# A running maximum for attention rows of over 1024 keys, with the rescale on GpSimd

## The chip, the core and the metric

The kernel runs on one core of a Trainium2 chip. A core has TensorE (PE in the profile; PEld is its weight load), VectorE (DVE), ScalarE (ACT), GpSimd (POOL) and SyncE (SP), which only issues transfers. The metric is the device time of one execution in microseconds. The kernel before takes 2585.28 us, the median of three runs (2584.13 to 2590.26). The profile was taken in an execution of its own, of 2582.51 us.

## What is computed

One layer of a hybrid encoder on 2048 tokens of width 1024, in float32: an attention branch and a gated linear recurrence on one projected input, merged by gates. The change touches the attention alone. It has 8 heads, 96 columns for queries and keys and 64 for values; a query sees all keys of its own chunk of 64 and of the earlier ones:

```python
sc = jnp.einsum('bhqd,bhkd->bhqk', qi, k).astype(jnp.float32) * scale
mask = key_chunk[None, :] <= qc[:, None]
sc = jnp.where(mask, sc, -jnp.inf)
p = jax.nn.softmax(sc, axis=-1).astype(v.dtype)
return jnp.einsum('bhqk,bhkd->bhqd', p, v)
```

## The kernel before

The kernel has five stages, one after another, with a barrier between them: input projection, merge logits and recurrence, the latent projections, attention, and merge with output. In each, every engine has its own written-out instruction list, and semaphores order them.

**Rows and chunks.** In `attention` a head's 2048 queries are 16 rows i of 128 queries each; four rows make a block b (TPB = 4, NB = 4). A row's keys come in chunks c of 512, b + 1 of them, the last cut at the diagonal. Rows 0 to 7 have up to 1024 keys and one piece of exponentials; rows 8 to 15 (blocks 2 and 3) have over 1024 keys and two pieces: piece 0 is chunks 0 and 1, 1024 columns, and piece 1 is the rest. LED = 8 is the first row with two pieces.

**One row.** TensorE (`queries`, L1651) computes each chunk of scores as three products of split operands (L66 to L68) into `scores`, which has four PSUM banks; before a chunk it waits until the piece that used this bank is exponentiated. VectorE (`maxima`, L1588) reduces each chunk to a column of `chunk_max` (L1592), these to `row_max` (L1595), and writes `neg_max` (L1601), the negative scaled maximum, into one of two columns by the parity of i. ScalarE (`exponentials`, L1530) waits for it before piece 0 (L1537), and writes exp(scale * score - maximum) to `probs[b]` in SBUF, with the sums of the piece in `sums` (L1541). Such an operation is followed in the profile by an ACTIVATION_READ_ACCUMULATOR, which delivers the sum.

**Tiles.** When a block's four rows are exponentiated, its probabilities are turned tile by tile: tile (b, j) is 128 keys by the block's queries. TensorE transposes it into one of three banks of `turn` (L1677), ScalarE rounds it into `pT` (`hi_part`, L1551), VectorE subtracts to get the low part (`lo_part`, L1608), and TensorE multiplies both by the values into `o_acc` (L1689, L1690). A finished block is copied to `oT` (L1565), turned (L1718), its halves are added (L1621), divided by the summed exponentials (`total`, `inv`) and stored (`o_out`, L1627).

**The order.** `attention_schedule` (L1358) gives 18 steps per head; each names a row, some tiles, a block to copy and a block to write out. Rows 8 to 11 go with the tiles of blocks 0 and 1, rows 12 to 15 with those of block 2, and rows 0 to 7 of the next head with those of block 3. In a step TensorE makes the row's scores, transposes this step's tiles and multiplies those of the step before; ScalarE rounds two tiles (AHEAD), does piece 0, rounds the rest and does piece 1; VectorE does the row's maxima, then the subtractions, then `outputs` of a block where there is one. The first tile of block 2, (2,0), is transposed in the step of row 12; that of block 3, (3,0), in the step of the next head's row 0, before which TensorE's scores of row 0 wait for all exponentials of this head. For block b, that first transpose waits for the last piece of the block's last row (L1673 to L1675). GpSimd only prepares two constants at the start of the stage and is then idle.

Of the kernel before, what the change touches and what calls it, by code (L numbers as in the profile page):

```python
# [7 lines left out]
ALU = mybir.AluOpType  # L8
ACT = mybir.ActivationFunctionType
# [4 lines left out]
P = 128  # L14
# [1364 lines left out]
def attention(nc, qT, knT, kpT, vTok, ident_d, oA):  # L1379
# [43 lines left out]
    with ExitStack() as ctx:  # L1423
# [19 lines left out]
        late_k = sb("late_k", [P, P], F32R)  # L1443
        mask_raw = sb("mask_raw", [P, 2, P])
        chunk_max = sb("chunk_max", [P, NB])
        row_max = sb("row_max", [P, 1])
        neg_max = sb("neg_max", [P, 2])
        sums = sb("sums", [P, NB, TPB, 2])
        total = sb("total", [P, TPB])
        inv = sb("inv", [P, TPB])  # L1450
# [11 lines left out]
        chunk_max_done = sem("chunk_max_done")  # L1462
        row_max_done = sem("row_max_done")
        max_ready = sem("max_ready")
        exp_done = sem("exp_done")
        turned = sem("turned")
        hi_ready = sem("hi_ready")
# [13 lines left out]
        with nc.Block() as block:  # L1481
# [37 lines left out]
            def _(pool):  # L1519
# [5 lines left out]
                pool.tensor_scalar(early_q[:], mask_raw[:, 0], 1.0, None, ALU.mult).then_inc(const_set, 1)  # L1525
                pool.tensor_scalar(late_k[:], mask_raw[:, 1], 1.0, None, ALU.mult).then_inc(const_set, 1)

            @block.scalar
            def _(act):
                def exponentials(h, i, piece):  # L1530
                    b, r = i // TPB, i % TPB
                    first, end = 2 * piece, min(2 * piece + 2, b + 1)
                    n = min(end * BLK, (i + 1) * P) - first * BLK
                    bank = s_bank(i, 0)
                    src = scores[:].rearrange("p b n -> p (b n)")[:, (bank + first) * BLK:(bank + first) * BLK + n]
                    if piece == 0:
                        act.wait_ge(max_ready, h * TT + (i + 1))  # L1537
                        if r == 0 and i < LED and not is_first(h):

                            act.wait_ge(turned, h * TURNS + (TURN_AT[b, TPB * (b + 1) - 1] + 1 - TURNS))  # L1540
                    act.activation(probs[b][:, r, first * BLK:first * BLK + n], src, ACT.Exp,  # L1541
                                   bias=neg_max[:, i % 2:i % 2 + 1], scale=SCALE,
                                   accum_out=sums[:, b, r, piece:piece + 1]).then_inc(exp_done, 1)

                def hi_part(h, tile):
# [41 lines left out]
            def _(dve):  # L1587
                def maxima(h, i):  # L1588
                    b = i // TPB
                    for c in range(b + 1):  # L1590
                        dve.wait_ge(qk_done, h * CHUNKS + (CHUNK_AT[i, c] + 1))
                        dve.reduce_max(chunk_max[:, c:c + 1], scores[:, s_bank(i, c), 0:width(i, c)], AX.X)\  # L1592
                           .then_inc(chunk_max_done, 1)
                    dve.wait_ge(chunk_max_done, h * CHUNKS + (CHUNK_AT[i, b] + 1))
                    dve.reduce_max(row_max[:], chunk_max[:, 0:b + 1], AX.X).then_inc(row_max_done, 1)  # L1595
                    dve.wait_ge(row_max_done, h * TT + (i + 1))
                    if not is_first(h) or i >= 2:
                        before = (i - 2) % TT
                        at = PIECE_AT[before, before // (2 * TPB)] - (PIECES if i < 2 else 0)
                        dve.wait_ge(exp_done, h * PIECES + (at + 2))  # L1600
                    dve.tensor_scalar(neg_max[:, i % 2:i % 2 + 1], row_max[:], -SCALE, None, ALU.mult).then_inc(max_ready, 1)  # L1601

                def lo_part(h, tile):
                    b, j = tile
# [6 lines left out]
                def outputs(h, b):  # L1611
                    at = TURN_AT["o", b]
                    n = h * NB + (b + 1)
                    if b >= 2:
                        dve.tensor_tensor(total[:], sums[:, b, :, 0], sums[:, b, :, 1], ALU.add).then_inc(total_ready, 1)
                    else:
                        dve.tensor_copy(total[:], sums[:, b, :, 0]).then_inc(total_ready, 1)
                    dve.wait_ge(total_ready, n)
                    dve.reciprocal(inv[:], total[:]).then_inc(inv_ready, 1)
                    dve.wait_ge(o_lo_ready, n)  # L1620
                    dve.tensor_tensor(o_sum[:], turn[:, at % 3].rearrange("p (t n) -> p t n", n=P)[:, :, 0:VD], o_lo[:],  # L1621
                                      ALU.add).then_inc(o_sum_ready, 1)
                    dve.wait_ge(o_sum_ready, n)
                    dve.wait_ge(inv_ready, n)
                    dve.sem_inc(turn_read, 1)
                    dve.wait_ge(o_stored[b % 2], h * 32 + (b // 2 * 16 + 16))
                    dve.tensor_tensor(o_out[:, b % 2], o_sum[:], inv[:].unsqueeze(2).to_broadcast([P, TPB, VD]), ALU.mult)\  # L1627
                       .then_inc(o_ready, 1)
# [21 lines left out]
            def _(pe):  # L1650
# [15 lines left out]
                def transposes(h, tile):  # L1666
# [6 lines left out]
                    if j == 0 or j >= TPB * b:  # L1673
                        i = TPB * b + (TPB - 1 if j == 0 else j - TPB * b)
                        pe.wait_ge(exp_done, h * PIECES + (PIECE_AT[i, i // (2 * TPB)] + 2))  # L1675
                    for r in range(max(0, j - TPB * b), TPB):
                        last = pe.transpose(turn[:, at % 3, r * P:(r + 1) * P], probs[b][:, r, j * P:(j + 1) * P], ident[:])  # L1677
                    last.then_inc(turned, 1)
# [478 lines left out]
```

## Time and profile before

| | before |
|---|---|
| median of three runs | 2585.28 us |
| profiled execution, span | 2582.51 us, 2580.7 us |
| mean granted TensorE clock | 0.943 |
| busy share PE, PEld, DVE, ACT, POOL | 88%, 73%, 44%, 35%, 16% |
| the attention stage's exponentials (L1541), first and last start | 1538.0 us, 2104.9 us |
| exponentials L1541 | 192, 166.9 us, 869 ns each |
| chunk maxima L1592 | 320, 184.0 us, 607 ns each |
| transposes L1677 | 1088, 152.7 us, 288 ns each |

The page gives for each group of instructions its line, engine, operation, the tile written and those read, the count, the busy time and the mean of one. "Idle before" is the time that the engine sat idle directly ahead of these instructions, with the one that ended it. Times in the rows by time are microseconds from the start of the span. Head 2's steps of rows 8 to 15 are at 1702 to 1745 us, and the other heads repeat them with nearly the same durations.

### The profile page before, as it was taken

How to read it: one execution, taken by the hardware profiler on the slowest of the kernel's cores; microseconds unless marked ns; L12 is line 12 of the kernel's file. 1: busy time of each engine (PE TensorE's matmuls, PEld its weight loads, DVE VectorE, ACT ScalarE, POOL GpSimd, SP SyncE). 2: the span in 40 equal slices, each digit the busy share in tenths (PEclk: the TensorE clock that was granted, in tenths of full speed). 3: DMA queues.
4: the chain of work that ended last, by engine and by line, in shares of the span. 5: the costliest groups of instructions: out<-in, count | busy, mean ns of one | idle time of the engine just before them, and what ended most of it. 6: DMA issues, size and time to landing. Idle time of an engine off the chain costs nothing. (4 is left out here: it accounts for less than half of the span.)

```text
span 2580.7 us, 34228 instructions
## 1 busy us (share of the span) xinstructions
PE 2275.6 (88%) x11680; PEld 1881.8 (73%) x11680; DVE 1127.4 (44%) x2016; ACT 911.7 (35%) x1676; POOL 423.4 (16%) x248
## 2 busy tenths in 40 slices
PE   6999999899699999999578948888888885889898
PEld 5888888688578888887456847777777764678776
DVE  5000000100044444444367746777777765554542
ACT  7111110101133433343441115555566653343431
POOL 1222241312011111111243200000000002411210
PEclk9999999999899999999679968999999996899999
DMA  5222221411222222221744460222221106563652
GB/s 177 74 73 73 73 77 33 147 69 53 87 80 93 89 90 93 89 90 62 243 148 132 116 175 12 64 65 63 65 62 36 39 10 225 165 182 123 192 160 68
DMA packets 228716, 256.06 MB, mean 99 GB/s; under 512 B 60272, under 2 KB 159344, under 8 KB 223728
## 3 DMA queue, kind: packets, MB, share of 16 engines
q1 hardware_dynamic: 203888, 208.11, 28.0%
q10 hardware_dynamic: 23616, 43.00, 4.4%
q0 software_dynamic: 1152, 4.19, 0.5%
q8 instruction: 32, 0.52, 0.1%
q14 instruction: 28, 0.23, 0.0%
HBM read 157.21 MB, written 98.04 MB: 99 GB/s over the span
## 5 line engine op out<-in xcount | busy, mean ns | idle before, releaser
L66 PE MATMUL bankD<-hT_hi,d_w_hi 128*128 128x512 f32 x512 | 213.0, 416 | 32.5 <-POOL d_w_lo L609 32.5
L1551 ACT ACTIVATE pT<-turn 128x512 fp32r<-128x512 f32 (+1 forms) x320 | 158.3, 532 | 198.5 <-PE turn L1677 198.1
L1608 DVE TENSOR_TENSOR pT<-turn,pT 128x512 fp32r<-128x512 f32 (+1 forms) x320 | 184.3, 606 | 73.8 <-ACT pT L1551 71.2
L66 PE MATMUL bankA<-hT_hi,w_hi 128*128 128x512 f32 x544 | 212.2, 390 | 0.0
L68 PE MATMUL bankA<-hT_hi,w_lo 128*128 128x512 f32 x544 | 211.7, 389 | 0.0
L67 PE MATMUL bankA<-hT_lo,w_hi 128*128 128x512 f32 x544 | 211.6, 389 | 0.0
L1592 DVE TENSOR_REDUCE chunk_max<-scores 128x1 f32<-128x512 f32 (+2 forms) x320 | 184.0, 607 | 59.7 <-PE scores L1663 44.5
L331 DVE TENSOR_TENSOR v_raw<-bankA,v_raw 128x512 fp32r<-128x512 f32 x16 | 11.0, 692 | 447.6 <-ACT v_raw L289 447.6
L66 PE MATMUL scores<-k_sb,q_sb 96*128 96x512 f32 (+2 forms) x320 | 130.3, 407 | 85.1 <-ACT probs L1541 48.4
L67 PE MATMUL bankD<-hT_lo,d_w_hi 128*128 128x512 f32 x512 | 201.7, 394 | 0.0
L68 PE MATMUL bankD<-hT_hi,d_w_lo 128*128 128x512 f32 x512 | 201.3, 393 | 0.0
L1541 ACT ACTIVATE probs<-scores,neg_max 128x1024 f32<-128x1024 f32 (+2 forms) x192 | 166.9, 869 | 44.2 <-DVE neg_max L1601 42.7
L66 PE MATMUL bankA<-wt_hi,hT_hi 128*128 128x512 f32 x384 | 153.0, 398 | 9.2 <-DVE v_raw L331 7.2
L1677 PE MATMUL turn<-ident_c,probs 128*128 128x128 f32 x1088 | 152.7, 288 | 1.7 <-ACT probs L1541 1.7
L67 PE MATMUL bankA<-wt_lo,hT_hi 128*128 128x512 f32 x384 | 151.3, 394 | 0.0
L68 PE MATMUL bankA<-wt_hi,hT_lo 128*128 128x512 f32 x384 | 151.3, 394 | 0.0
L66 PEld LDWEIGHTS scores<-k_sb,q_sb 96*128 96x128 f32 x320 | 64.1, 200 | 115.7 <-ACT probs L1541 64.1
L271 ACT ACTIVATE stage<-bankA 128x512 f32<-128x512 f32 x68 | 40.7, 598 | 301.6 <-PE bankA L68 300.1
L66 PEld LDWEIGHTS bankD<-hT_hi,d_w_hi 128*128 128x128 f32 x512 | 97.0, 189 | 56.5 <-issue 20.7
L1689 PE MATMUL o_acc<-pT,v_sb 128*128 128x512 f32 (+1 forms) x320 | 128.9, 406 | 8.8 <-ACT oT L1565 5.7
L66 PE MATMUL bankE<-e_uT,e_wb_hi 128*128 128x512 f32 x256 | 105.3, 411 | 31.4 <-POOL e_wb_lo L1888 29.8
L1677 PEld LDWEIGHTS turn<-ident_c,probs 128*128 128x128 f32 x1088 | 127.1, 149 | 4.3 <-DVE pT L1608 2.3
(224 smaller groups left out, 4925.6 us busy)
## 6 DMA issues: line engine op xcount, KB each, us to landing
projT<-stage ACTq DMA_DIRECT2D x68, 256.0 KB, 2.4
projT<-d_stage ACTq DMA_DIRECT2D x64, 256.0 KB, 2.4
e_l_in<-projT SPq DMA_DIRECT2D x64, 256.0 KB, 4.6
qT<-out_b SPq DMA_DIRECT2D x64, 192.0 KB, 2.2
q_sb<-qT SPq DMA_DIRECT2D x16, 768.0 KB, 10.3
w_raw<-in_w_in_dram SPq DMA_DIRECT2D x16, 512.0 KB, 4.5
hgTok<-v_raw SPq DMA_DIRECT2D x16, 512.0 KB, 2.6
gateTok<-stage ACTq DMA_DIRECT2D x32, 256.0 KB, 2.0
```

The source lines that it names most:

```text
L66: pe.matmul(out, a_hi, b_hi, start=first, stop=False)
L67: pe.matmul(out, a_hi, b_lo, start=False, stop=False)
L68: return pe.matmul(out, a_lo, b_hi, start=False, stop=last)
L271: act.activation(stage[:, blk], src, func).then_inc(bank_free, 1)
L331: dve.tensor_tensor(v_out[:, t % 2, :, 1], bank[:, t % 8].rearrange("p (h n) -> p h n", n=VD), v_out[:, t % 2, :, 0].bitcast(F32), ALU.sub ...
L1541: act.activation(probs[b][:, r, first * BLK:first * BLK + n], src, ACT.Exp, bias=neg_max[:, i % 2:i % 2 + 1], scale=SCALE, accum_out=sums[ ...
L1551: act.activation(pT[:, at % RING, 0, r0 * P:], turn[:, TURN_AT[tile] % 3, r0 * P:], ACT.Copy)\
L1592: dve.reduce_max(chunk_max[:, c:c + 1], scores[:, s_bank(i, c), 0:width(i, c)], AX.X)\
L1608: dve.tensor_tensor(pT[:, at % RING, 1, r0 * P:], turn[:, TURN_AT[tile] % 3, r0 * P:], pT[:, at % RING, 0, r0 * P:].bitcast(F32), ALU.subt ...
L1677: last = pe.transpose(turn[:, at % 3, r * P:(r + 1) * P], probs[b][:, r, j * P:(j + 1) * P], ident[:])
L1689: pe.matmul(dst, v_sb[:, u, j], pT[:, at % RING, 0, r0 * P:], start=j == 0, stop=False)
```

## The change

Rows 8 to 15 get a maximum per piece. After the first two chunks VectorE writes row_max and neg_max of piece 0 and ScalarE may exponentiate piece 0 by it. After the remaining chunks a second row_max, over all chunks, gives the neg_max of piece 1. ScalarE then computes `early_scale`, the exponential of the difference of the two, one column, ahead of piece 1. GpSimd multiplies the piece 0 of `probs` in place by it, 1024 columns, one instruction per row. TensorE's first transpose of blocks 2 and 3 waits for the rescales of the block's rows, and `outputs` multiplies the first sum by the scale before adding the second.

```diff
@@ gpsimd
+                with pool.Fori(0, HEADS) as h:
+                    for i in range(LED, TT):
+                        b, r = i // TPB, i % TPB
+                        pool.wait_ge(scale_ready, h * (TT - LED) + (i - LED + 1))
+                        pool.sem_inc(waited_pool, 1)
+                        pool.tensor_scalar(probs[b][:, r, 0:2 * BLK], probs[b][:, r, 0:2 * BLK], early_scale[:, b, r:r + 1], None,
+                                           ALU.mult).then_inc(rescaled, 1)
@@ scalar, exponentials
-                    if piece == 0:
-                        act.wait_ge(max_ready, h * TT + (i + 1))
+                    act.wait_ge(max_ready, h * PIECES + (PIECE_AT[i, piece] + 1))
+                    if piece == 1:
+                        act.activation(early_scale[:, b, r:r + 1], neg_max[:, i % 2, 0:1], ACT.Exp,
+                                       bias=neg_max[:, i % 2, 1:2], scale=-1.0).then_inc(scale_ready, 1)
+                    else:
                         if r == 0 and i < LED and not is_first(h):
 
                             act.wait_ge(turned, h * TURNS + (TURN_AT[b, TPB * (b + 1) - 1] + 1 - TURNS))
                     act.activation(probs[b][:, r, first * BLK:first * BLK + n], src, ACT.Exp,
-                                   bias=neg_max[:, i % 2:i % 2 + 1], scale=SCALE,
+                                   bias=neg_max[:, i % 2, piece:piece + 1], scale=SCALE,
@@ vector, maxima
-                    for c in range(b + 1):
...
+                    for piece in range(b // 2 + 1):
+                        end = min(2 * piece + 2, b + 1)
+                        for c in range(2 * piece, end):
+                            dve.wait_ge(qk_done, h * CHUNKS + (CHUNK_AT[i, c] + 1))
+                            dve.reduce_max(chunk_max[:, c:c + 1], scores[:, s_bank(i, c), 0:width(i, c)], AX.X)\
+                               .then_inc(chunk_max_done, 1)
+                        dve.wait_ge(chunk_max_done, h * CHUNKS + (CHUNK_AT[i, end - 1] + 1))
+                        dve.reduce_max(row_max[:, piece:piece + 1], chunk_max[:, 0:end], AX.X).then_inc(row_max_done, 1)
+                        dve.wait_ge(row_max_done, h * PIECES + (PIECE_AT[i, piece] + 1))
...
+                        dve.tensor_scalar(neg_max[:, i % 2, piece:piece + 1], row_max[:, piece:piece + 1], -SCALE, None, ALU.mult)\
+                           .then_inc(max_ready, 1)
@@ vector, outputs
                     if b >= 2:
-                        dve.tensor_tensor(total[:], sums[:, b, :, 0], sums[:, b, :, 1], ALU.add).then_inc(total_ready, 1)
+                        dve.tensor_tensor(total[:], sums[:, b, :, 0], early_scale[:, b], ALU.mult).then_inc(early_sum, 1)
+                        dve.wait_ge(early_sum, h * 2 + (b - 1))
+                        dve.tensor_tensor(total[:], total[:], sums[:, b, :, 1], ALU.add).then_inc(total_ready, 1)
@@ tensor, transposes
                         pe.wait_ge(exp_done, h * PIECES + (PIECE_AT[i, i // (2 * TPB)] + 2))
+                    if j == 0 and b >= 2:
+                        pe.wait_ge(rescaled, h * (TT - LED) + (b - 1) * TPB)
```

The order of the instructions themselves changes at these places. VectorE, the maxima of a row of block 3 (four chunks), before:

```order
L1592 TENSOR_REDUCE chunk_max<-scores 128x1
L1591 REGISTER_ALU
L1592 TENSOR_REDUCE chunk_max<-scores 128x1
L1591 REGISTER_ALU
L1592 TENSOR_REDUCE chunk_max<-scores 128x1
L1591 REGISTER_ALU
L1592 TENSOR_REDUCE chunk_max<-scores 128x1
L1595 TENSOR_REDUCE row_max<-chunk_max 128x1
L1596 REGISTER_ALU
L1600 REGISTER_ALU
L1601 TENSOR_SCALAR neg_max<-row_max 128x1
```

And the same row in the change (the REGISTER_ALU rows compute the value of a wait):

```order
L1610 TENSOR_REDUCE chunk_max<-scores 128x1
L1609 REGISTER_ALU
L1610 TENSOR_REDUCE chunk_max<-scores 128x1
L1613 TENSOR_REDUCE row_max<-chunk_max 128x1
L1614 REGISTER_ALU
L1619 TENSOR_SCALAR neg_max<-row_max 128x1
L1609 REGISTER_ALU
L1610 TENSOR_REDUCE chunk_max<-scores 128x1
L1609 REGISTER_ALU
L1610 TENSOR_REDUCE chunk_max<-scores 128x1
L1613 TENSOR_REDUCE row_max<-chunk_max 128x1
L1619 TENSOR_SCALAR neg_max<-row_max 128x1
```

A row_max and a neg_max stand after the second chunk, ahead of the third and the fourth. ScalarE in the step of row 14, from piece 0 to piece 1, before:

```order
L1541 ACTIVATE probs,sums<-scores,neg_max 128x1024
L1549 REGISTER_ALU
L1550 REGISTER_ALU
L1551 ACTIVATE pT<-turn 128x512
L1541 ACTIVATE probs,sums<-scores,neg_max 128x896
```

And in the change:

```order
L1557 ACTIVATE probs,sums<-scores,neg_max 128x1024
L1565 REGISTER_ALU
L1566 REGISTER_ALU
L1567 ACTIVATE pT<-turn 128x512
L1549 REGISTER_ALU
L1551 ACTIVATE early_scale<-neg_max 128x1
L1557 ACTIVATE probs,sums<-scores,neg_max 128x896
```

The one-column exponential stands between the third tile and piece 1. TensorE in the change, from the last chunk of the next head's row 0 (L1684 is its mask product) to the first tiles of block 3:

```order
L1684 MATMUL scores<-late_k,early_q 128x128
L1693 REGISTER_ALU
L1696 REGISTER_ALU
L1698 REGISTER_ALU
L1700 MATMUL turn<-ident_c,probs 128x128 x4
L1693 REGISTER_ALU
L1700 MATMUL turn<-ident_c,probs 128x128 x4
L1712 MATMUL o_acc<-pT,v_sb 128x384
```

The matmuls keep their order; the third register row (L1698) is the new wait for GpSimd ahead of the four transposes of tile (3,0).

## Rows read from the trace of the kernel before

**Rows 1.** Waits in 1500 to 2125 us: total, times, longest (us).
```profile
PE scores L66 <- ACT probs L1541: 48.4, 33, 1.9
ACT pT L1551 <- PE turn L1677: 198.1, 133, 3.9
```

**Rows 2.** Groups by shape, 1500 to 2125 us: busy us, mean ns, idle before.
```profile
L1541 ACT ACTIVATE probs<-scores,neg_max 128x1024 f32<-128x1024 f32 x80 | 89.2, 1115 | 11.6 <-DVE neg_max L1601 10.7
```

**Rows 3.** ScalarE by time, rows 14, 15: start, length, line, operation, idle.
```profile
1735.29 1.09 ACT L1551 ACTIVATE pT<-turn 128x512 fp32r<-128x512 f32 x2 [1.89 <-PE turn L1677]
1737.22 1.11 ACT L1541 ACTIVATE probs<-scores,neg_max 128x1024 f32<-128x1024 f32 x1 [0.85 <-DVE neg_max L1601]
1738.23 0.19 ACT L1541 ACTIVATION_READ_ACCUMULATOR probs<-scores,neg_max 128x1 f32 x1
1738.81 1.01 ACT L1541 ACTIVATE probs<-scores,neg_max 128x896 f32<-128x896 f32 x1
...
1744.18 1.11 ACT L1541 ACTIVATE probs<-scores,neg_max 128x1024 f32<-128x1024 f32 x1
```

**Rows 4.** TensorE by time: tile (2,0); row 15's chunks; tile (3,0).
```profile
1722.14 0.84 PE L1677 MATMUL turn<-ident_c,probs 128*128 128x128 f32 x6
...
1738.48 0.50 PE L66 MATMUL scores<-k_sb,q_sb 96*128 96x512 f32 x1 [1.05 <-ACT probs L1541]
...
1739.97 0.48 PE L66 MATMUL scores<-k_sb,q_sb 96*128 96x512 f32 x1
...
1745.99 1.72 PE L1677 MATMUL turn<-ident_c,probs 128*128 128x128 f32 x7
```

**Rows 5.** ScalarE by time, row 11: rounded tiles, piece 0, piece 1.
```profile
1717.45 0.77 ACT L1551 ACTIVATE pT<-turn 128x384 fp32r<-128x384 f32 x2 [1.75 <-PE turn L1677]
1718.31 1.12 ACT L1541 ACTIVATE probs<-scores,neg_max 128x1024 f32<-128x1024 f32 x1
...
1719.58 0.69 ACT L1541 ACTIVATE probs<-scores,neg_max 128x512 f32<-128x512 f32 x1
```

**Rows 6.** VectorE by time, maxima and subtractions of row 14.
```profile
1734.37 2.35 DVE L1592 TENSOR_REDUCE chunk_max<-scores 128x1 f32<-128x512 f32 x4
1736.75 0.16 DVE L1595 TENSOR_REDUCE row_max<-chunk_max 128x1 f32<-128x4 f32 x1
1737.03 0.15 DVE L1601 TENSOR_SCALAR neg_max<-row_max 128x1 f32<-128x1 f32 x1
...
1738.95 0.69 DVE L1608 TENSOR_TENSOR pT<-turn,pT 128x512 fp32r<-128x512 f32 x1 [0.56 <-ACT pT L1551]
```

**Rows 7.** ScalarE line of another stage: ns min/median/max, first, last.
```profile
L1968 ACT ACTIVATE e_std<-e_ss,e_eps x16: 294/295/296, 2247.6 to 2573.4; 128x1 f32<-128x1 f32 x16
```

**Rows 8.** GpSimd groups: tensor_scalar at 1024 and 128, memset at 1024.
```profile
L207 POOL TENSOR_SCALAR w_hi<-w_raw 128x1024 fp32r<-128x1024 f32 x17 | 47.1, 2773 | 282.7 <-PE bankA L68 271.2 <-DMA w_raw<-in_w_in_dram 11.1 <-POOL w_lo L209 0.4
L1525 POOL TENSOR_SCALAR early_q<-mask_raw 128x128 fp32r<-128x128 f32 x1 | 0.5, 532 | 0.1
L597 POOL MEMSET d_masked<- 128x1024 f32 x1 | 1.0, 951 | 0.0
```

**Rows 9.** ScalarE, GpSimd, VectorE by time, last stage.
```profile
2181.69 1.04 ACT L1926 ACTIVATE e_wb_hi<-e_wb_raw 128x1024 fp32r<-128x1024 f32 x1
...
2182.82 2.35 POOL L1888 TENSOR_TENSOR e_wb_lo<-e_wb_raw,e_wb_hi 128x1024 fp32r<-128x1024 f32 x1 [3.42 <-ACT e_wb_hi L1926]
...
2185.14 2.82 POOL L1901 TENSOR_TENSOR e_wo_lo<-e_y,e_wo_hi 128x1024 fp32r<-128x1024 f32 x1
...
2185.76 2.75 DVE L1990 TENSOR_TENSOR e_u<-e_sg,e_o_in 128x512 f32<-128x512 f32 x1
```

**Rows 10.** GpSimd and VectorE by time, latent projections.
```profile
1404.76 2.13 POOL L1131 TENSOR_SCALAR wq_hi<-wq_raw 128x768 fp32r<-128x768 f32 x1 [12.26 <-PE bankB L68]
...
1404.78 1.34 DVE L1284 TENSOR_TENSOR out_b<-turned,out_b 96x512 fp32r<-96x512 f32 x1 [0.70 <-ACT out_b L1211]
```

**Rows 11.** The stretch after row 15: length, busy by engine, granted clock.
```profile
1745.40:1749.00 3.60, 3.56 (x18) 3.57 (x19) 1.62 (x5) 1.20 (x2) 0.00 (x0) 0.56 0.00 0
```

More of the change, by code:

```diff
@@ L1445, in attention @@
         chunk_max = sb("chunk_max", [P, NB])
-        row_max = sb("row_max", [P, 1])
-        neg_max = sb("neg_max", [P, 2])
+        row_max = sb("row_max", [P, 2])
+        neg_max = sb("neg_max", [P, 2, 2])
+        early_scale = sb("early_scale", [P, NB, TPB])
         sums = sb("sums", [P, NB, TPB, 2])
@@ L1464, in attention @@
         max_ready = sem("max_ready")
+        scale_ready = sem("scale_ready")
+        rescaled = sem("rescaled")
+        early_sum = sem("early_sum")
+        waited_pool = sem("waited_pool")
         exp_done = sem("exp_done")
@@ L1589, in maxima @@
                     b = i // TPB
-                    for c in range(b + 1):
[L1591 to L1601, printed above, removed]
+                    for piece in range(b // 2 + 1):
[7 more added lines that the diff above has]
+                        dve.wait_ge(row_max_done, h * PIECES + (PIECE_AT[i, piece] + 1))
+                        if piece == 0 and (not is_first(h) or i >= 2):
+                            before = (i - 2) % TT
+                            at = PIECE_AT[before, before // (2 * TPB)] - (PIECES if i < 2 else 0)
+                            dve.wait_ge(exp_done, h * PIECES + (at + 2))
+                        dve.tensor_scalar(neg_max[:, i % 2, piece:piece + 1], row_max[:, piece:piece + 1], -SCALE, None, ALU.mult)\
+                           .then_inc(max_ready, 1)
                 def lo_part(h, tile):
```

## Prediction

> **What bounds the kernel now.** The page puts TensorE at 88% of the span, and its slices 24 to 33 are the attention stage, the only place that the change touches. I first read who waited for whom in that stage, then the groups by shape, then the time-ordered rows of one head (head 2, counted from 0, 1702 to 1775 us).
>
> The waits [rows 1] say that TensorE's own idle time there is short and comes mostly from ScalarE's exponentials (48.4 us), while ScalarE waits 198.1 us for transposes. Nobody holds the stage alone; a loop does. In each step TensorE makes the scores of row i, then transposes; ScalarE rounds two transposed tiles, exponentiates piece 0 of row i, and only that frees the banks for row i+1. The rows of head 2 show it: TensorE's first score matmul of row 15 starts at 1738.48 [rows 4], 0.06 us after ScalarE's piece 0 of row 14 ended at 1738.42 [rows 3].
>
> Does that piece wait for the maximum, which is what the change shortens? Seldom. Of all exponentials 1024 wide, 80 of them, ScalarE idled 10.7 us for neg_max in total [rows 2], and row 14 of one head alone has 0.85 us of it [rows 3], so 6.8 us over eight heads. Row 7's exponential is also 1024 wide and its code is unchanged. In row 11 the tile before ends at 1718.22 and the piece starts at 1718.31 [rows 5]. In the other rows over 1024 keys the piece starts when ScalarE itself is free.
>
> **What the change saves.** In row 14 VectorE is late, because it has just written out a block. Its four reduces take 2.35 us from 1734.37, so the spacing is 0.55 and the second ends at 1735.61; row_max follows after 0.04 and neg_max ends 0.43 after that starts [rows 6]: 1736.08 instead of 1737.18. ScalarE's second rounded tile ends at 1736.38, and ScalarE starts an operation 0.10 us and more before the last one ends (the accumulator read starts at 1738.23, the exponential ends at 1738.33) [rows 3]. With 0.12 for that, piece 0 could start at 1736.26, 0.96 us earlier. Other heads lose slightly less; I take 0.90. Row 11 can give 0.20 by the same overlap. Eight heads: 8 x 1.10 = 8.8 us gained, at best.
>
> **What it adds on ScalarE.** One exponential of one column before each piece 1. Its kind is not in this stage; the 128x1 activation elsewhere takes 295 ns [rows 7], less the 0.12 overlap 0.18 us. Bounds: 0.09 (a 0.19 us accumulator read less an overlap of 0.10) and 0.30. In row 14 piece 1 frees the third bank just in time: it starts at 1738.81, takes 1.01 and an accumulator read of 0.19, and the third chunk starts at 1739.97 [rows 3, 4]. There it costs 0.16 x 8 = 1.3 us. In rows 8 to 13 piece 1 is narrower and its end leaves TensorE room. In row 15 it is inside the next term.
>
> **What it adds on VectorE.** A row_max and a neg_max in the middle of each of 64 rows: 0.04 + 0.43 less 0.08 overlap and 0.09 that the next reduce would have overlapped, 0.48 us a row, 31 us in all. It is hidden: the piece 0 no longer waits for what comes after it, and after the two subtractions VectorE idles 0.56 us for the third tile [rows 6]. If that cover were gone it would cost at most those 31 us. The extra add for the sums of blocks 2 and 3 is two operations and a wait, 0.28 us; in block 2 it delays rows 2 and 3, whose exponentials VectorE does hold, but ScalarE then waits for transposes anyway: 1 us in total, bounds 0 and 2.2.
>
> **What it adds on GpSimd, and through it on TensorE.** This is the term that decides. Each of 64 rows gets one GpSimd tensor_scalar of 128x1024 float32. The nearest rows are exactly that operation and size, only into fp32r and with a constant: 2773 ns each, and 0.53 us at 128 columns [rows 8], that is 2.5 ns a column. I take 2.77. From below the nearest is the memset of 1024 columns, 0.95 us [rows 8]; from above I know nothing that excludes more for the per-row scalar, and put 3.3 as an estimate (the row plus a fifth).
>
> GpSimd was empty here, so 48 of the 64 have steps of time to spare: TensorE waits for them only at tile 0 of blocks 2 and 3, for rows 8 to 11 and 12 to 15. What decides is the last row of each, 16 in all. The chain is: scale ends 0.12 after piece 1 starts, GpSimd starts 0.09 later (as after ScalarE's rounding, 2182.73 to 2182.82) [rows 9], 2.77, and 0.06 to TensorE: 3.04 us after piece 1 starts, and piece 1 itself starts 0.18 later than now.
> Row 15: piece 1 starts at 1744.18 [rows 3] and the transposes of tile (3,0) at 1745.99 [rows 4], 1.81 us later. Late by 0.18 + 3.04 - 1.81 = 1.41 us, 8 times: 11.3 us.
> Row 11: piece 1 starts at 1719.58 [rows 5], the transposes of tile (2,0) at 1722.14 [rows 4], 2.56 us later. Late by 0.66 us, 8 times: 5.3 us.
> Queued behind the waiting transpose are all of TensorE's other transposes and value products of that step; ScalarE and VectorE wait for those. I find no later wait that gives it back.
>
> The GPSIMD Engine Reference of the Trainium skill, section 4.1 (Engine selection), says that a one-input operation on GpSimd is roughly line-rate. By that rule the rescale would take about 1.1 us as an estimate and both lateness terms would vanish. The 2773 ns row speaks against it.
>
> **A shared port.** VectorE operations that read two SBUF tensors are held by GpSimd here: e_u 128x512 took 2.75 us, ending 0.55 after GpSimd's own operation (2187.96) [rows 9], where 512 columns else take 0.69 [rows 6]. Under a GpSimd tensor_scalar it is shorter: out_b started 0.02 after wq_hi and ended at 1406.12, when wq_hi still ran until 1406.89 [rows 10]. Reduces and the subtractions read PSUM and are not in that class. In the change the small copy of the sums and o_out of block 1 come within 2.5 us after row 13's piece 1 starts, so they fall into row 13's rescale. I take 0.5 us of delay for VectorE, of which row 14's new slack covers 0.18: 0.3 x 8 = 2.6 us of the gain is lost. Bounds 0 and 7.7 (all of row 14's gain).
> SBUF — State Buffer of the Trainium skill, section Who interferes with whom, says the loser blocks for the whole instruction. By it the delay would be near 1.3 us and the loss 7.7; the out_b row contradicts it for a GpSimd tensor_scalar.
>
> **The clock.** After the idle time before row 0 of head 3 the granted clock was 0.56 in 1745.4 to 1749, most of it at the lower level, 1.2 GHz [rows 11]. The idle ahead of it grows by 1.4 us, so more heads may see the lower level there. Such a stretch costs up to half of its 3.6 us; I add 3 us, bounds 0 and 8.
>
> **Sum.** 11.3 + 5.3 + 1.3 + 2.6 + 1.0 + 3.0 - 8.8 = +15.7 us. The profiled execution took 2582.51 us, so 2598.2; the median of the runs is 2.8 above it, so 2601. About 0.3% (7.8 us) is what a measurement can tell from no change.
>
> **Rivals.**
> A: the rescale is short enough to be hidden (1.0 to 1.8 us). For it: the memset runs at 0.93 ns a column, and the output is plain float32, not fp32r. Against it: both sizes of the same operation, at 2.5 ns a column. Then no lateness and no port trouble: 1.4 (row 15's scale) + 1.3 + 1.0 - 8.8 = -5.1, or 2580. This is also the case on the other side: faster if the mechanism at row 14 gives its whole 0.96 us; it decides as soon as the rescale is under about 1.6 us (1.81 less 0.18 is what TensorE leaves). With 2.0 to 2.3 us it comes out within 0.3%, some 2583 to 2587.
> B: VectorE becomes the late one. Held until the rescale's end in the copy and again in o_out, it would start row 14's reduces over 2 us late, and piece 0 of row 14 would wait longer than now. Then +7.7 - 2.6 and up to 8 more for the later start: 2606 to 2614. For it: the held operations [rows 9, 10]. Against: out_b's early release.
> C: the change does not do what it says, since piece 0 is held by ScalarE's order and not by the maximum. For rows 8, 9, 10, 12 and 13 that is so, and it is in the forecast. Were it so in row 14 too, the gain of 7.2 us would be gone and with it the 2.6 lost from it: 2606.
>
> **Chances.** Forecast 0.58 (its own range 2592 to 2609), A 0.20, a rescale in between 0.12, B 0.10. Of the forecast 0.06 falls within 0.3%, all of the in-between does, and of A two thirds. Faster 0.07, same 0.31, slower 0.62. The range 2580 to 2611 leaves out half of A and the end of B.
>
> **What would show it.** In the profile after: a group of 64 GpSimd tensor_scalars, near 2770 ns; TensorE waiting on GpSimd 16 times, 0.6 to 0.7 us in eight and 1.4 in eight, at the transposes; ScalarE's neg_max wait in row 14 gone or down to 0.3; 64 one-column activations near 0.3 us. Wrong if the GpSimd group is under 1.9 us, if the transposes do not wait for it, or if VectorE's o_out is held beyond a microsecond.

## The result, and the profile after

| | before | after |
|---|---|---|
| median (range), 5 runs each | 2584.13 us (2578.39 to 2590.26) | 2608.89 us (2607.30 to 2610.63) |
| ratio | | 1.0098, 95% interval 1.0082 to 1.0113 |
| profiled execution, span | 2582.51 us, 2580.7 us | 2608.89 us, 2607.1 us |
| mean granted TensorE clock | 0.943 | 0.938 |
| busy share of GpSimd | 16% | 23% |

The change makes the kernel slower by 24.8 us, where 15.7 us were forecast: 2608.9 us instead of 2601. That lies 0.1 us inside the forecast's own range (2592 to 2609) and in the wider one (2580 to 2611). The sign, the place and the mechanism are as forecast; one term, the clock, was much larger and lies outside its own bounds.

**The groups that the change adds or moves.** First the page of the profile after (line, engine, operation, tile, count, busy us, mean ns, idle before):

```profile
L1538 POOL TENSOR_SCALAR probs<-probs,early_scale 128x1024 f32<-128x1024 f32 x64 | 182.2, 2846 | 432.2 <-ACT early_scale L1551 432.2
```

Then the groups by shape in 1500 to 2125 us, which answer [rows 2]:

```profile
L1557 ACT ACTIVATE probs<-scores,neg_max 128x1024 f32<-128x1024 f32 x79 | 88.3, 1118 | 3.6 <-DVE neg_max L1619 3.6
L1551 ACT ACTIVATE early_scale<-neg_max 128x1 f32<-128x1 f32 x63 | 19.3, 306 | 0.0
L1619 DVE TENSOR_SCALAR neg_max<-row_max 128x1 f32<-128x1 f32 x192 | 29.5, 154 | 10.0 <-DVE row_max L1613 1.1
```

The rescale (GpSimd's multiplication of piece 0) takes 2.85 us, near the 2.77 taken from the operation of the same size [rows 8]. ScalarE's idle time for the maximum ahead of a 1024-wide piece fell from 10.7 to 3.6 us: the change does what it says. The waits of the same stretch (total us, times, longest), against [rows 1]:

```profile
PE scores L66 <- ACT probs L1557: 41.5, 30, 1.8
PE turn L1700 <- POOL probs L1538: 14.2, 15, 1.3
PEld turn L1700 <- POOL probs L1538: 13.2, 12, 1.4
```

The last two are new: TensorE waits for GpSimd. The two are the matmul's and the weight load's sides of the same waits, not to be added. One by one the 16 waits are 0.62 to 0.75 us ahead of tile (2,0), 1.24 to 1.31 us ahead of tile (3,0), and 3.73 us in the last head.

**One wait, step by step.** ScalarE, GpSimd and TensorE by time in head 2, row 15 and the next head's row 0 (start us, length us; the counterparts are [rows 3] and [rows 4]):

```profile
1748.88 1.12 ACT L1557 ACTIVATE probs<-scores,neg_max 128x1024 f32<-128x1024 f32 x1
1749.88 0.21 ACT L1557 ACTIVATION_READ_ACCUMULATOR probs<-scores,neg_max 128x1 f32 x1
1749.97 0.29 ACT L1567 ACTIVATE pT<-turn 128x128 fp32r<-128x128 f32 x1
1750.13 0.31 ACT L1551 ACTIVATE early_scale<-neg_max 128x1 f32<-128x1 f32 x1
1750.31 1.13 ACT L1557 ACTIVATE probs<-scores,neg_max 128x1024 f32<-128x1024 f32 x1
...
1750.64 2.84 POOL L1538 TENSOR_SCALAR probs<-probs,early_scale 128x1024 f32<-128x1024 f32 x1 [2.57 <-ACT early_scale L1551]
...
1751.59 0.33 PE L66 MATMUL scores<-k_sb,q_sb 96*128 96x128 f32 x1 [1.76 <-ACT probs L1557]
1751.98 0.32 PE L1684 MATMUL scores<-late_k,early_q 128*128 128x128 f32 x1
1753.54 1.97 PE L1700 MATMUL turn<-ident_c,probs 128*128 128x128 f32 x8 [1.24 <-POOL probs L1538]
1755.16 0.67 PE L1712 MATMUL o_acc<-pT,v_sb 128*128 128x384 f32 x1
```

The scale ends at 1750.44, GpSimd starts 0.20 later (0.09 was forecast), ends at 1753.48, and the transposes start 0.06 after that: 3.23 us after the start of piece 1, where 1.81 were spent before. Note the lengths at the end: transposes of about 0.25 us each, at half speed.

**The clock there.** Windows of TensorE (length; busy by engine; the granted clock is the third number from the end), row 14, row 15, rows 0 and 1 of the next head, and the whole low stretch; they answer [rows 11]:

```profile
1738.56:1744.41 5.85, 5.71 (x35) 4.56 (x33) 5.16 (x12) 3.96 (x10) 2.85 (x1) 1.00 0.10 22
1744.41:1751.59 7.18, 5.42 (x26) 3.95 (x26) 6.00 (x15) 4.91 (x12) 3.80 (x2) 1.00 0.00 0
1751.59:1756.69 5.10, 3.86 (x18) 3.67 (x19) 1.73 (x5) 1.19 (x2) 1.89 (x1) 0.55 0.00 0
1756.69:1760.38 3.69, 3.69 (x22) 3.46 (x22) 2.00 (x6) 2.56 (x7) 0.00 (x0) 0.70 0.00 0
...
1752.00:1758.80 6.80, 5.56 (x27) 5.38 (x26) 2.71 (x8) 2.21 (x6) 1.48 (x1) 0.50 0.00 0
```

TensorE idles 1.76 us ahead of row 0's scores and another 1.24 us at the wait, and 6.8 us run at 1.2 GHz. Rows 0 and 1 of the same head before, 6.41 us instead of 8.79:

```profile
1745.43:1749.11 3.68, 3.67 (x19) 3.68 (x19) 1.74 (x5) 1.20 (x2) 0.00 (x0) 0.56 0.00 0
1749.11:1751.84 2.73, 2.73 (x22) 2.51 (x22) 1.79 (x6) 2.39 (x7) 0.00 (x0) 0.97 0.00 0
```

Before, a stretch of 3.4 us at half speed followed row 15 in four of seven heads and none in three; after, one of 6.8 us in each of the seven.

**Where the time went.** From the timeline, each row's step is the time from its first score matmul to the next row's. Summed over the heads (row 15: seven heads, since the last has no successor), in us. The first head's rows 0 to 7 stand ahead of the loop, without tiles; of its rows 0 and 1, 1.8 us are in each number of "0+1". "Half" is the time in the stage at the lower clock, 21 to 28 us of it in the stage's first rows in every kernel. This table also holds the experiments of the next section.

| kernel | stage | 8+9 | 12 | 13 | 14 | 15 | 0+1 | 7 | half |
|---|---|---|---|---|---|---|---|---|---|
| before | 563.2 | 87.0 | 52.9 | 48.6 | 52.8 | 48.7 | 41.7 | 42.1 | 69.8 |
| after | 584.1 | 83.4 | 59.3 | 50.4 | 46.7 | 50.4 | 64.3 | 41.5 | 100.6 |
| 1 scratch | 561.9 | 86.0 | 52.6 | 53.6 | 46.6 | 50.3 | 43.3 | 41.4 | 82.5 |
| 2 operations only | 567.8 | 88.7 | 53.1 | 48.9 | 58.6 | 50.7 | 35.4 | 41.4 | 58.6 |
| 3 split rescale | 560.0 | 87.4 | 52.6 | 53.6 | 46.4 | 50.4 | 40.1 | 41.4 | 79.6 |
| 4 filler at the wait | 582.0 | 82.4 | 59.2 | 58.2 | 46.4 | 50.3 | 55.3 | 41.5 | 86.2 |
| 5 kept busy | 579.6 | 92.6 | 59.3 | 55.2 | 46.5 | 50.3 | 45.8 | 41.5 | 86.8 |
| 6 row 14 only | 561.9 | 86.0 | 52.9 | 50.3 | 45.5 | 51.0 | 44.9 | 42.1 | 79.4 |
| 7 all but 11, 15 | 568.0 | 87.7 | 52.9 | 52.1 | 47.0 | 52.0 | 44.9 | 42.1 | 85.4 |
| 8 before, fillers | 566.1 | 92.1 | 52.9 | 45.5 | 52.9 | 48.6 | 35.4 | 49.1 | 55.8 |
| 9 split, fillers | 567.9 | 93.3 | 60.6 | 45.1 | 46.7 | 50.3 | 35.4 | 47.9 | 56.2 |
| 10 row 14, fillers | 560.3 | 88.5 | 52.9 | 45.5 | 45.4 | 51.0 | 35.4 | 51.9 | 51.4 |
| 11 row 14, one filler | 560.3 | 93.7 | 52.9 | 50.3 | 45.5 | 51.0 | 35.4 | 42.1 | 77.7 |

After less before: row 12 +6.4, rows 0 and 1 +22.6, row 15 +1.7, row 13 +1.8, row 14 -6.1, row 11 -1.0, rows 8 and 9 -3.6, the rest -0.9: +20.9. Behind the last row 15 the kernel takes 487.6 us where it took 481.4; the last head's wait is in that. In experiments 1, 2, 3 and 6 to 11, which have no such wait or a shorter one, it is 480.8 to 484.7, so some 3 us of the 6.2 can be scatter.

### The profile page after: what moved, and what is told of

It reads as the page before. It is cut to its first block and busy times, and to the rows that moved or that the text cites. A ratio compares the mean times of both kernels' runs of the same rounds, so it can differ in the third digit from the quotient of the medians.

```text
span 2607.1 us, 34783 instructions
## 1 busy us (share of the span) xinstructions
PE 2292.2 (88%) x11680; PEld 1893.3 (73%) x11680; DVE 1152.1 (44%) x2160; ACT 921.7 (35%) x1740; POOL 606.2 (23%) x312
## 5 line engine op out<-in xcount | busy, mean ns | idle before, releaser
L1538 POOL TENSOR_SCALAR probs<-probs,early_scale 128x1024 f32<-128x1024 f32 x64 | 182.2, 2846 | 432.2 <-ACT early_scale L1551 432.2
L66 PE MATMUL scores<-k_sb,q_sb 96*128 96x512 f32 (+2 forms) x320 | 131.6, 411 | 78.6 <-ACT probs L1557 41.5
L1700 PE MATMUL turn<-ident_c,probs 128*128 128x128 f32 x1088 | 161.6, 299 | 17.9 <-POOL probs L1538 17.9
L1700 PEld LDWEIGHTS turn<-ident_c,probs 128*128 128x128 f32 x1088 | 134.1, 155 | 22.6 <-POOL probs L1538 13.2
L1911 POOL TENSOR_TENSOR e_wb_lo<-e_wb_raw,e_wb_hi 128x1024 fp32r<-128x1024 f32 x32 | 76.1, 2379 | 293.0 <-ACT e_wb_hi L1949 293.0
```

Source lines behind the costliest of these rows:

```text
L66: pe.matmul(out, a_hi, b_hi, start=first, stop=False)
L1538: pool.tensor_scalar(probs[b][:, r, 0:2 * BLK], probs[b][:, r, 0:2 * BLK], early_scale[:, b, r:r + 1], None, ALU.mult).then_inc(rescaled, 1)
L1911: pool.tensor_tensor(wb_lo[:, u], wb_raw[:, u], wb_hi[:, u].bitcast(F32), ALU.subtract).then_inc(wb_ready, 1)
```

## Experiments

**Is it the wait? (1 scratch).** GpSimd does the same multiplications but writes to a buffer of its own, so piece 0 is not rescaled; TensorE's wait moves from a block's first tile to its fifth, where it is long over. GpSimd also waits for its own last multiplication (not shown).

```diff
-   pool.tensor_scalar(probs[b][:, r, 0:2 * BLK], probs[b][:, r, 0:2 * BLK], early_scale[...], None, ALU.mult)
+   pool.tensor_scalar(scaled_c[:], probs[b][:, r, 0:2 * BLK], early_scale[...], None, ALU.mult)
-   if j == 0 and b >= 2:
+   if j == TPB and b >= 2:
```

> The change with GpSimd's products written to a buffer of their own (so piece 0 isn't rescaled), and TensorE's wait for them moved from tile 0 to tile 4 of blocks 2 and 3. All instructions of the change remain, only nobody waits. Theory W (TensorE's 16 waits for the last rows' rescales, and the lower clock that follows them, are the whole loss): 3 to 7 us faster than before (row 14's 0.8 us in eight heads, less some 1.5 us of ScalarE's extra operation), the clock after row 15 as before. Rival P (GpSimd holds VectorE on the shared port, and the 31 us of added VectorE work come through): still at least 8 us slower than before.

Measured: 2581.03 us against 2586.46 for before on the same chip, ratio 0.9975 (0.9965 to 0.9985), inside theory W's 3 to 7 us. All of ScalarE's, VectorE's and GpSimd's new work is there, and the kernel is faster than before:

```profile
L1541 POOL TENSOR_SCALAR scaled_c<-probs,early_scale 128x1024 f32<-128x1024 f32 x64 | 182.0, 2844 | 410.9 <-ACT early_scale L1554 410.9
L1554 ACT ACTIVATE early_scale<-neg_max 128x1 f32<-128x1 f32 x64 | 19.6, 306 | 0.0
```

So the loss hangs on TensorE's wait for the rescale and what follows from it, and not on the added instructions by themselves; what the shared port costs is within the gain that is left. The multiplications are not in place here, which leaves it open whether that matters; their length, 2844 ns, is the same.

**What is the earlier start worth? (2 operations only).** As 1, but piece 0 waits for the row's last maximum again.

```diff
-   act.wait_ge(max_ready, h * PIECES + (PIECE_AT[i, piece] + 1))
+   act.wait_ge(max_ready, h * PIECES + (PIECE_AT[i, i // (2 * TPB)] + 1))
```

> As the kernel with the products in a buffer of their own, but piece 0 waits for the row's last maximum, so that the added operations remain and the early start is gone; output wrong in the same way. Theory W: against that kernel later by the early start at row 14, which is now 0.8 us plus VectorE's added 0.5 us and the held copy's 0.7 us, eight times: 8 to 16 us; against before +3 to +10 us. If the early start were worth nothing (rival C of the prediction), both kernels would be equal within 3 us.

Measured: 2595.12 us, ratio 1.0035 (1.0022 to 1.0049), inside both ranges of theory W: 14.1 us later than 1, 8.7 later than before. The row of the 1024-wide pieces:

```profile
L1560 ACT ACTIVATE probs<-scores,neg_max 128x1024 f32<-128x1024 f32 x80 | 89.1, 1114 | 18.4 <-DVE neg_max L1622 17.9
```

17.9 us of idle time for the maximum instead of 3.6, and row 14 takes 58.6 us instead of 46.6. The added operations are free only because the earlier start covers them: without it they make row 14 5.8 us longer than before, with it the row is 6.2 shorter. The 14 us between 1 and 2 are both together. Experiment 2 shows something of the clock too: TensorE idles 1.8 us ahead of row 0's scores as in the other kernels, and yet no half-speed stretch follows in any of the seven heads (rows 0 and 1: 35.4 us). The length of that idle time alone does not decide.

**Can the wait be avoided? (3 split rescale).** For rows 11 and 15 the rescale is cut in two, 384 and 640 columns; tile 0 waits for the first, tile 3 for the second. Everything is computed.

```diff
-   pool.tensor_scalar(probs[b][:, r, 0:2 * BLK], ...).then_inc(rescaled, 1)
+   for c0, c1 in ((0, 3 * P), (3 * P, 2 * BLK)) if r == TPB - 1 else ((0, 2 * BLK),):
+       pool.tensor_scalar(probs[b][:, r, c0:c1], probs[b][:, r, c0:c1], ...).then_inc(rescaled, 1)
-   if j == 0 and b >= 2:
-       pe.wait_ge(rescaled, h * (TT - LED) + (b - 1) * TPB)
+   if j in (0, 3) and b >= 2:
+       pe.wait_ge(rescaled, h * 2 * (TPB + 1) + (b - 2) * (TPB + 1) + (TPB if j == 0 else TPB + 1))
```

> The change with the rescale of rows 11 and 15 cut in two, 384 and 640 columns; tile 0 waits for the first part alone, tile 3 for the second. The first part takes about 1.2 us (2.5 ns a column and 0.2), ends 1.5 us after piece 1 starts, ahead of both tiles. Theory W: all waits go, 3 to 7 us faster than before. Rival P: at least 8 us slower than before.

Measured: 2581.85 us, ratio 0.9987 (0.9976 to 0.9999), 3.4 us by the ratio, as theory W had it. The parts take 1.24 and 1.89 us (1.2 was expected for the first). GpSimd by time at the same place as above, the waits of TensorE for it:

```profile
1742.85 3.10 POOL L1539 TENSOR_SCALAR probs<-probs,early_scale 128x384 f32<-128x384 f32 x2 [2.57 <-ACT early_scale L1552]
```

```profile
PE turn L1701 <- POOL probs L1539: 2.1, 1, 2.1
```

One wait is left of sixteen, the last head's, which has no scores of a next row 0 ahead of it (3.73 us in the change); row 12 is back at 52.6 us and rows 0 and 1 at 40.1. The same arithmetic with a shorter first instruction turns +24.8 us into a gain of 0.1%, less than the 0.3% that the prediction took for the least that a measurement tells; the interval here, of 11 runs against 21, just leaves out no change.

**How much is the clock? (4 filler at the wait, 5 kept busy).** Fillers are transposes of the identity into the bank that the step's first tile overwrites. Experiment 4 puts 6 (block 2) or 10 (block 3) ahead of the wait for GpSimd:

```diff
    if j == 0 and b >= 2:
+       for n in range(10 if b == 3 else 6):
+           pe.transpose(turn[:, at % 3, n % TPB * P:(n % TPB + 1) * P], ident[:], ident[:])
        pe.wait_ge(rescaled, h * (TT - LED) + (b - 1) * TPB)
```

> The change with TensorE filling its wait for GpSimd: 6 transposes of the identity at tile (2,0), 10 at tile (3,0), into the bank that the tile's own transposes overwrite. The waits stay as long, the idle time ahead of the tiles goes. Theory W with the clock as its larger half: the half-speed stretches after row 15 (6.8 us in each head) go or halve, 7 to 14 us faster than the change, +11 to +18 us against before. Rival (the stretches come from other idle time, such as that ahead of row 0's scores, or cost nothing): like the change, +25 us.

Measured: 2604.92 us, ratio 1.0074 (1.0062 to 1.0086): 0.24% below the change's 1.0098, the expectation's lower edge not reached. The half-speed stretch after row 15 became 3.4 us instead of 6.8, and rows 0 and 1 fell by 9.0 us. But row 13 rose by 7.8, since a half-speed stretch now fell there in every head:

```profile
1730.31:1737.54 7.23, 7.23 (x35) 6.11 (x36) 5.00 (x11) 3.73 (x9) 2.85 (x1) 0.76 0.00 0
```

Experiment 5 keeps the ten at block 3 only and adds 12 ahead of row 0's scores, so that both idle times around row 0 are filled (the ten are not shown again).

```diff
+   if i in (0,) and at is not None:
+       pe.wait_ge(turn_read, h0 * TURNS + (at - 1))
+       for m in range(12):
+           pe.transpose(turn[:, at % 3, m % TPB * P:(m % TPB + 1) * P], ident[:], ident[:])
```

> The changed kernel with TensorE kept busy in its two idle stretches around the end of row 15: 12 identity transposes ahead of the scores of the next head's row 0 and 10 ahead of the wait for GpSimd at tile (3,0), into the bank that this step's first tile overwrites. The rescale and both waits stay. Theory K (the piece of the loss that the forecast sized too small is the half-speed stretch that follows the longer idle, about 1.8 us a head of the 3.2 us by which rows 0 and 1 grew): those rows fall from 8.9 us to about 7.0 to 7.2 in every head that has both fillers, and the kernel takes 12 to 16 us less than the change, 2593 to 2597, unless another row turns to half speed. Rival L (the loss is the wait itself): rows 0 and 1 stay at 8.9 us and the time within 4 us of the change, 2605 or more.

Measured: 2600.29 us, ratio 1.0047 (1.0031 to 1.0062). TensorE by time, then rows 0 and 1 as windows:

```profile
1746.09 1.53 PE L1679 MATMUL turn<-ident_c 128*128 128x128 f32 x12 [0.28 <-DVE pT L1627]
1747.59 0.33 PE L66 MATMUL scores<-k_sb,q_sb 96*128 96x128 f32 x1
...
1748.09 1.28 PE L1703 MATMUL turn<-ident_c 128*128 128x128 f32 x10
1749.54 1.09 PE L1707 MATMUL turn<-ident_c,probs 128*128 128x128 f32 x8 [0.17 <-POOL probs L1538]
```

```profile
1747.58:1751.23 3.65, 3.48 (x30) 3.24 (x29) 0.89 (x4) 0.92 (x2) 1.90 (x1) 1.00 0.00 0
1751.23:1753.88 2.65, 2.65 (x23) 2.42 (x22) 2.46 (x7) 2.56 (x8) 0.00 (x0) 1.00 0.00 0
```

The wait is still there, its end still set by GpSimd, and eight transposes now take 1.09 us instead of 1.97. Rows 0 and 1 take 6.29 us a head instead of 8.79 (head 2 to 3), the same within 0.02 us in all seven heads; in the table 45.8 against 64.3 us. That is below the 7.0 to 7.2 expected. With the wait unchanged and the clock at 1.00, 18.5 us of the change's time in these rows was the lower clock. The stage as a whole is only 4.5 us shorter, because rows 8 and 9 rose by 9.2 and row 13 by 4.8, to half-speed stretches there: row 13 has one in six of eight heads instead of three. By the ratios the kernel gained 0.51%, by the medians of two chips 8.6 us. The theory that the clock is the missing part holds for the rows it names; its number for the whole, 2593 to 2597, was missed for the reason it had reserved.

**Which rows carry the gain? (6 row 14 only, 7 all but 11 and 15).** The running maximum is restricted to some rows; the others have one maximum and no rescale.

```diff
+ RUNNING = (14,)
...
-   for i in range(LED, TT):
+   for i in RUNNING:
...
-   for piece in range(b // 2 + 1):
+   for piece in range(b // 2 + 1 if i in RUNNING else 1):
```

> The change for row 14 alone: the other rows over 1024 keys have one maximum for both pieces as before, and block 2 has no rescale. Theory W: row 14's start 0.8 us earlier in eight heads, less 0.1 for ScalarE's operation, and no wait for GpSimd: 4 to 7 us faster than before. Rival (the early start is given back in row 15): within 2 us of before.

Measured: 2581.78 us against 2586.21 for before (second chip), ratio 0.9985 (0.9974 to 0.9997), 4 us as theory W had it. Eight of the 64 running maxima give as much as all of them with the split rescale (0.9987): row 14 takes 45.5 us instead of 52.8. A part goes to row 15, +2.3, and to rows 13, 0 and 1.

With `RUNNING = (8, 9, 10, 12, 13, 14)`:

> The running maximum for rows 8, 9, 10, 12, 13 and 14; rows 11 and 15, the last of their blocks, keep one maximum and need no rescale. Theory W (the loss sits in the rescales of the last rows alone, and the other rows' operations are hidden): the gain at row 14 stays, and the time is that of the split rescale, 2579 to 2584. Rival Q (the operations of all rows cost something that a late rescale hid): 2586 or more.

Measured: 2590.48 us against 2587.48 (third chip), ratio 1.0009 (0.9999 to 1.0018). Rival Q's number came, not W's. The row of the 1024-wide pieces shows one reason:

```profile
L1565 ACT ACTIVATE probs<-scores,neg_max 128x1024 f32<-128x1024 f32 x80 | 89.2, 1115 | 6.7 <-DVE neg_max L1627 5.7
```

The 2.1 us above the change's 3.6 are row 15, some 0.30 a head: it now waits for a maximum over all four chunks, while VectorE comes late from row 14's additional operations. Against experiment 3, row 15 is 1.6 us longer, row 11 1.1, and rows 0 and 1 4.8, these by the clock. The running maximum of the other rows has no gain of its own in this table, and row 14's operations delay VectorE for row 15.

**Can the clock be had back by itself? (8 to 11).** 12 fillers each ahead of the scores of rows 0, 9 and 13, where TensorE idled before, put into the kernel before, into 3 and into 6; at last into 6 ahead of row 0 alone. The edit is that of experiment 5, with `i in (0, 9, 13)` for 8 to 10.

> The kernel before, with 12 transposes of the identity on TensorE ahead of the scores of rows 0, 9 and 13, where it idles 1.7 us in every head; they write the bank that the next tile overwrites. Theory W with its clock part (half-speed stretches follow these idles, 0.9 us a head after row 15, 1.0 at row 9 and 0.4 at row 13): 8 to 20 us faster than before, granted clock 0.955 or more. Rival (the stretches have another cause, or the fillers delay TensorE): no faster than before.

Measured: 2582.66 us, ratio 0.9982 (0.9969 to 0.9995), 3.6 us faster where 8 to 20 were expected, with a granted clock of 0.950 where 0.955 or more was: a miss in size. Rows 0, 1, 9 and 13 are at full clock in nearly all heads; rows 0 and 1 are the reference for full speed, 4.82 us a head:

```profile
1746.07:1748.23 2.16, 2.16 (x18) 2.16 (x19) 0.89 (x4) 0.92 (x2) 0.00 (x0) 1.00 0.00 0
1748.23:1750.89 2.66, 2.66 (x23) 2.43 (x22) 2.46 (x7) 2.57 (x8) 0.00 (x0) 1.00 0.00 0
```

They saved 6.3 us in rows 0 and 1, 10.3 in row 9 and 3.1 in row 13, and lost 15.4 in row 8 and 7.0 in row 7. TensorE by time at the end of row 7 of head 4, and the window of row 8:

```profile
1840.90 0.66 PE L1722 MATMUL turn<-ident_c,oT 128*128 128x128 f32 x4 [0.72 <-ACT oT L1565]
1845.54 0.79 PE L66 MATMUL scores<-k_sb,q_sb 96*128 96x512 f32 x1 [3.97 <-issue]
```

```profile
1845.54:1853.49 7.95, 7.52 (x32) 6.54 (x32) 3.56 (x8) 2.81 (x7) 0.00 (x0) 0.54 0.98 221
```

TensorE stood 3.97 us without any wait that the profile shows ("issue"), where the loop over the heads turns, and 4.41 us at the turn before (head 2), and ran at half speed after it. In this one profiled execution the stage is 2.9 us longer than before, while the median of 12 runs is 3.6 below that of 35: the rows tell where the time moves, not how large the whole is in other executions. What holds TensorE there was not tried.

> The rescale of rows 11 and 15 cut in two, and the same 12 transposes ahead of rows 0, 9 and 13. Theory W: the two gains add, 12 to 25 us faster than before.

Measured: 2588.24 us, ratio 1.0011 (1.0000 to 1.0022), a clear miss. To the losses in rows 7 and 8 comes row 12, 60.6 us instead of 52.6: the fillers ahead of row 13's scores wait for VectorE to read their bank, and that comes 1.49 us after TensorE's last product instead of 0.50 in experiment 8, so they end too late. TensorE by time at the end of head 3's row 12:

```profile
1798.06 1.53 PE L1680 MATMUL turn<-ident_c 128*128 128x128 f32 x12 [1.49 <-DVE pT L1628]
1799.34 0.48 PE L66 MATMUL scores<-k_sb,q_sb 96*128 96x512 f32 x1
```

VectorE is later there by the added row_max and neg_max and by o_out, 0.81 us instead of 0.43, of which below.

> The running maximum for row 14 alone, and the same 12 transposes ahead of rows 0, 9 and 13. Theory W: the two gains add, 12 to 26 us faster than before, as the split one or slightly better.

Measured: 2580.91 us, ratio 0.9976 (0.9964 to 0.9987), 5.3 us faster where 12 to 26 were expected. A miss in size too; row 7 takes 51.9 us, with 5.5 us of TensorE standing at each of the two turns.

> The running maximum for row 14 alone, with 12 identity transposes ahead of the scores of row 0 only; none ahead of rows 9 and 13. With the fillers ahead of rows 0, 9 and 13 in the kernel before, rows 7 and 8 grew by more than 1 us a head; theory M: that is the longer instruction list at the loop's turn and half speed there, so a third of the fillers keeps rows 0 and 1 at 4.8 us and leaves rows 7 and 8 near 5.6 and 4.8: 7 us less than row 14 alone, about 2575. Rival N: any filler moves the half-speed stretch to another row, and the time stays near 2581.

Measured: 2578.98 us against 2587.48, ratio 0.9966 (0.9953 to 0.9979). With a third of the fillers row 7 is back at 42.1 us, as theory M had it, and rows 0 and 1 keep their 35.4; rows 8 and 9 rose to 93.7 by half-speed stretches there, which is rival N's. The time lies between theory M's 2575 and rival N's 2581. It is the fastest complete version run, faster than both kernels (its profiled execution, 2585.30, was its slowest); against 6 alone the intervals overlap.

## Why the prediction was right, and where its size was off

The chain that it put first, the two last rescales that TensorE waits for, is what the runs show. That the total lies within the range owes something to the range's width: the clock term alone is 7.4 us above its forecast.

**The rescale's price.** 2.77 taken, 2.85 measured. Rival A, the short rescale, fails by it. The estimate of 1.1 us by the rule of the GPSIMD Engine Reference of the Trainium skill, section 4.1 (Engine selection), fails too, against 2.85.

**Lateness of rows 11 and 15.** Forecast 0.66 and 1.41 us a head, 16.6 in all. Row 12's step grew by 0.80 a head, 6.4 in all. For row 15 the clean measure is experiment 5 against 8, both at full clock: 3.65 us against 2.16 in row 0, 1.49 a head, 11.9 for eight. Together 18.3. The chain was right link by link; only GpSimd's start (0.20 for 0.09) and its length were short.

**ScalarE's scale.** 0.306 us ([rows 7] have 0.295) with 0.13 of it overlapped: piece 1 starts 0.22 after the end of piece 0's accumulator read instead of 0.06. Forecast 1.3 us; row 15's step is 1.7 longer in seven heads.

**The gain, and the shared port.** Forecast -7.2 in row 14 and -1.6 in row 11, with 2.6 given back to the port: -6.2. Measured -6.1 and -1.0: -7.1. VectorE by time, between the subtractions and row 14's maxima, answers [rows 6]; GpSimd's rescale runs from 1739.27 to 1742.12:

```profile
1739.53 0.88 DVE L1638 COPY total<-sums 128x4 f32<-128x4 f32 x1
1740.44 0.18 DVE L1640 RECIPROCAL inv<-total 128x4 f32<-128x4 f32 x1
...
1741.11 0.43 DVE L1648 TENSOR_TENSOR o_out<-o_sum,inv 128x256 f32<-128x256 f32 x1 [0.19 <-DVE o_sum L1642]
1741.46 1.28 DVE L1610 TENSOR_REDUCE chunk_max<-scores 128x1 f32<-128x512 f32 x2
1742.77 0.15 DVE L1613 TENSOR_REDUCE row_max<-chunk_max 128x1 f32<-128x2 f32 x1
1742.96 0.15 DVE L1619 TENSOR_SCALAR neg_max<-row_max 128x1 f32<-128x1 f32 x1
1743.06 1.16 DVE L1610 TENSOR_REDUCE chunk_max<-scores 128x1 f32<-128x512 f32 x2
```

The copy was held, 0.88 us instead of 0.16; o_out was not, 0.43 us in the middle of the rescale. It also matters when they start. In all eight heads block 1's copy starts 0.26 us after the rescale's start and ends 1.13 to 1.14 us after it; block 0's copy ends as its rescale starts and takes 0.16. In experiment 3 o_out of block 0 starts 0.17 to 0.25 us after the start of the 640-column part, and there it is held too, in all eight heads, until 1.07 us after that start. GpSimd, then VectorE, in experiment 3:

```profile
1717.41 3.10 POOL L1539 TENSOR_SCALAR probs<-probs,early_scale 128x384 f32<-128x384 f32 x2 [1.51 <-ACT early_scale L1552]
1718.89 0.81 DVE L1649 TENSOR_TENSOR o_out<-o_sum,inv 128x256 f32<-128x256 f32 x1 [0.27 <-DVE o_sum L1643]
```

In the change neg_max ends at 1743.11 and piece 0 starts at 1743.15, right behind ScalarE's rounded tiles: the delay just fitted in. In experiment 6, where row 13 is not rescaled and the copy takes 0.16 us, row 14 takes 45.5 us over the heads instead of 46.7: the held copy costs at most 1.2 us, where 2.6 were forecast. Rival B, VectorE as the late one, fails. The rule that the loser blocks for the whole instruction (SBUF — State Buffer of the Trainium skill, section Who interferes with whom) agrees with neither row: the copy was let go 1.72 us before the rescale's end. Rival C fails in row 14: without the earlier start it takes 12 us more (experiments 1 and 2).

**The clock: the step that was mis-sized.** The prediction put "3 us, bounds 0 and 8" for more heads at the lower level; measured are 10.4, outside these bounds. Rows 0 and 1 lost 6.3 us to it before (41.7 less 35.4 at full speed, experiment 8) and 18.5 after (64.3 less 45.8, experiment 5): +12.2 in seven heads. Rows 8 and 9 gave back 3.6, and row 13 added 1.8: 10.4 us in all, from one profiled execution of each kernel. How many heads have a stretch after row 15 varies without the wait as well: rows 0 and 1 lose between nothing (experiment 2) and 9.5 us (6) to it. The working reckoned with one stretch of 3.6 us as in [rows 11], in more heads, and capped it at half of its length. It took the new wait for a longer idle time ahead of the stretch ("grows by 1.4 us"). It is a second one, of 1.24 us, that comes four matmuls, 0.7 us, after the first one of 1.76. With both the stretch is 6.8 us in all seven heads, where four of seven had one of 3.4; with the second one filled (experiment 4) it is 3.4 us in all seven, with both filled (5) there is none.

**The sum by rows of the trace.** Lateness 18.3, clock 10.4, scale 1.9, gain -7.1, small rows -0.9: +22.6, and the scatter behind the stage. The terms forecast were 16.6, 3.0, 1.3, -6.2 and +1.0 for the outputs. The last did not show: rows 2 to 6 have the same steps as before within 0.02 us.

What stays open: why an idle time of 1.8 us is followed by a half-speed stretch in some heads and not in others, why the stretches move to rows 8, 9 and 13 when they are filled at row 0, and what holds TensorE at the loop's turn in experiment 8.

## What to carry to other kernels

Of 64 hidden operations the two a head whose consumer comes next decided; look for the last one before each consumer, and cut it so that what is read first is done first (24.8 us lost against 3 to 5 gained, with the same arithmetic). An idle time of TensorE that stands close to another one can cost more than its length: here 1.49 us of wait a head brought another 1.7 us lost to the lower clock. Restrict such a change to the rows that wait for what it shortens: eight of 64 gave as much as all with the split rescale.

## What the runs showed of the hardware

- A GpSimd multiplication of 128x1024 float32 in place by a per-row scalar takes 2.84 to 2.85 us, the same into another buffer; 384 and 640 columns take 1.24 and 1.89 us, 3.10 together.
- VectorE's copy of 128x4 and its product of two 128x256 SBUF operands were held when they started 0.17 to 0.26 us after such a multiplication, in every case: 0.88 us instead of 0.16 and 0.81 to 0.90 instead of 0.43. Both were let go 1.07 to 1.14 us after its start, also where it ran to 2.85. The product was not held when it started 1.39 us or more after it, reduces of scores from PSUM were not at 0.25 us, nor was the reciprocal of 128x4 at 0.05 and 1.17 us, nor row_max at 0.76 (experiment 3).
- TensorE's idle time of 1.7 us ahead of row 0's scores was followed by 3.4 us at 1.2 GHz in four of seven heads before; one of 1.8 us in experiment 2 by none in seven; 1.76 and then 1.24 us, 0.7 us apart, by 6.8 us in all seven.
- 22 identity transposes a head, kept in TensorE's idle time, brought rows 0 and 1 from 8.79 to 6.29 us, with the same wait in them. In all six kernels with fillers the lower clock then appeared in rows where it had not been, or longer.
